# Stick-breaking attention: the third key tile's value product as three rounded products, and the values of heads 5 and 7 one slot later

## The reference

```python
def _stick_breaking(cols):                       # cols: 512 x 3072, eight heads of width 128
    q = _heads(cols[..., :MIX_WIDTH], SB_HEADS, SB_HEAD_DIM) * (SB_HEAD_DIM ** -0.5)
    k, v = ...
    for i in range(seq // BLOCK_Q):              # blocks of 128 queries, keys up to the block's end
        z = jnp.einsum('bhqd,bhkd->bhqk', qb, k[:, :, :end]).astype(jnp.float32)
        u = jnp.where(mask, jax.nn.softplus(z), 0.0)
        a = jnp.where(mask, jnp.exp(z - _rev_cumsum(u)), 0.0)
        outs.append(jnp.einsum('bhqk,bhkd->bhqd', a.astype(v.dtype), v[:, :, :end]))
```

## Time and profile before

| | |
|---|---|
| median of 3 runs | 2968.88 us (2968.79 to 2970.55) |
| the profiled execution | 2968.38 us, its span 2966.7 us |
| PE busy | 2950.7 us, 99% of the span |
| DVE busy | 2253.9 us, 76% |
| ACT busy | 1470.8 us, 50% |
| mean granted clock of PE | 0.999 of full speed |

### The profile page before, as it was taken

How to read it: one execution, slowest core, us unless ns; L and a number is a source line. 1 busy time by engine, 2 the same in 40 slices (tenths; PEclk the granted TensorE clock), 3 DMA queues, 4 the chain that set the end, 5 groups by cost and what they waited for, 6 DMA issues and landing times.

```text
span 2966.7 us, 47938 instructions
## 1 busy us (share of the span) xinstructions
PE 2950.7 (99%) x18733; PEld 2649.9 (89%) x18733; DVE 2253.9 (76%) x2781; ACT 1470.8 (50%) x2158; POOL 60.9 (2%) x148
## 2 busy tenths in 40 slices
PE   9999999999999999999999999999999999999999
PEld 8779999888889999878899998889999888899998
DVE  7979888567659887576598875558898567588884
ACT  4576555455445555344455553226555354365554
POOL 6100000000000000000000000000000000000000
PEclk9999999999999999999999999999999999999999
DMA  6232333341133333311332333223233322233332
GB/s 204 60 96 87 112 113 107 107 142 58 55 101 100 102 104 106 101 57 56 101 100 99 106 101 107 85 71 114 99 102 104 93 85 66 63 114 99 108 98 79
DMA packets 261943, 286.45 MB, mean 97 GB/s; under 512 B 12514, under 2 KB 233888, under 8 KB 261800
## 3 DMA queue, kind: packets, MB, share of 16 engines
q1 hardware_dynamic: 261688, 284.42, 29.9%
q10 hardware_dynamic: 112, 0.02, 0.0%
HBM read 280.21 MB, written 5.78 MB: 96 GB/s over the span
## 4 chain that ended last, share of the span: by engine, by line
PE 93%; DVE 4%; POOL 1%; ACT 1%; issue 1%; DMA 0%; ACTq 0%; POOLq 0%; DVEq 0%; SPq 0%
PE ps L2961 40%; PE ps L2612 14%; PE ps L2614 14%; PE ps L2613 14%; PE ps L3323 1%; PE ps L3324 1%; PE ps L3325 1%; PE ps L3230 1%; PE ps L3290 1%; PE ps L3269 1%; PE ps L3309 1%; PE ps L3311 1%; PE ps L3310 1%; PE ps L3176 1%; PE ps L3165 0%
## 5 line engine op out<-in xcount | busy, mean ns | idle before, releaser
L869 ACT ACTIVATE whi<-raw 128x2048 fp32r<-128x2048 f32 (+2 forms) x144 | 246.5, 1712 | 472.6 <-PE ps L2614 382.4
L1559 DVE TENSOR_TENSOR wlo<-raw,whi 128x2048 fp32r<-128x2048 f32 (+2 forms) x144 | 293.5, 2038 | 220.8 <-ACT whi L869 220.5
L2961 PE MATMUL ps<-th,wh 128*128 128x256 f32 x1600 | 453.7, 284 | 0.6 <-DVE wl L1648 0.5
L2961 PE MATMUL ps<-tl,wh 128*128 128x256 f32 x1600 | 452.7, 283 | 0.0
L2961 PE MATMUL ps<-th,wl 128*128 128x256 f32 x1600 | 452.7, 283 | 0.0
L2612 PE MATMUL ps<-hh,whi 128*128 128x512 f32 x896 | 356.2, 398 | 0.0
L2614 PE MATMUL ps<-hh,wlo 128*128 128x512 f32 x896 | 349.5, 390 | 0.0
L2613 PE MATMUL ps<-hl,whi 128*128 128x512 f32 x896 | 349.2, 390 | 0.0
L2961 PE MATMUL ps<-hh,wh 128*128 128x256 f32 x1200 | 340.1, 283 | 0.1
L2961 PE MATMUL ps<-hh,wl 128*128 128x256 f32 x1200 | 339.6, 283 | 0.0
L2961 PE MATMUL ps<-hl,wh 128*128 128x256 f32 x1200 | 339.6, 283 | 0.0
(11 more groups left out here) (517 smaller groups left out, 6674.4 us busy)
## 6 DMA issues: line engine op xcount, KB each, us to landing
raw<-in_w_ffn_in SPq DMA_DIRECT2D x88, 1024.0 KB, 5.1
raw<-in_w_in SPq DMA_DIRECT2D x59, 1024.0 KB, 5.3
raw<-in_w_ffn_out SPq DMA_DIRECT2D x40, 1024.0 KB, 5.1
raw<-in_w_o SPq DMA_DIRECT2D x32, 640.0 KB, 4.4
raw<-in_w_gate SPq DMA_DIRECT2D x11, 1024.0 KB, 5.4
raw<-in_w_up SPq DMA_DIRECT2D x11, 1024.0 KB, 5.3
raw<-in_w_down SPq DMA_DIRECT2D x10, 1024.0 KB, 5.1
raw<-in_w_out SPq DMA_DIRECT2D x4, 1024.0 KB, 5.1
```

The source lines that it names most:

```text
L869: a.activation(whi[:, slot, 0:n], raw[:, slot, 0:n], ACT.Copy).then_inc(hi_made, 1)
L1559: v.tensor_tensor(wlo[:, u % 2, 0:n], raw[:, u % 2, 0:n], whi[:, u % 2, 0:n].bitcast(F32), ALU.subtract).then_inc(lo_made, 1)
L2961: e = mm(bank(b, HALF), wgt[:, q, w], xx, start=start and k == 0 and m == 0, stop=k == KD // 2 - 1 and m == 2, skip_group_check=True)
```

## The change

The places of the third and the fourth key tile change, so that the third one lies next to the first two; sticks_hi and sticks_lo grow from 896 to 1152 columns and sticks_t shrinks from 384 to 128; v_hi and v_lo hold three key tiles' values in place of two; and the third tile's product goes through `three`. ACT's v_hi so needs all of the pair's values (`values_taken(h // 2, 1)`). sticks_lo and v_lo lie in other places of SBUF. In the table KPV, the fifth head goes from slot 41 to 42, and the seventh from 53 to 54.

```diff
-ZK = {0: 0, 1: 512, 3: 896, 2: 1024}
+ZK = {0: 0, 1: 512, 2: 896, 3: 1152}
...
-KPV = [25, 29, 33, 37, 41, 45, 53, 56]
+KPV = [25, 29, 33, 37, 42, 45, 54, 56]
...
-        sticks_lo = at("sticks_lo", US0, [P, WIDE], F32R)
+        sticks_lo = at("sticks_lo", GS0 + 3072, [P, WIDE], F32R)
...
-        v_hi = at("v_hi", SQB0, [P, 2, 256], F32R)
-        v_lo = at("v_lo", SQB0 + 2048, [P, 2, 256], F32R)
+        v_hi = at("v_hi", SQB0, [P, 3, 256], F32R)
+        v_lo = at("v_lo", GS0, [P, 3, 256], F32R)
...
-                        act.wait_ge(acc_free, g_in(3 * idx) + values_taken(h // 2, 0))
+                        act.wait_ge(acc_free, g_in(3 * idx) + values_taken(h // 2, 1))
...
-                        a.activation(v_hi[:, :, :], vp[h // 2 % 2][:, 0:2, :], ACT.Copy).then_inc(S("v_hi"), 1)
+                        a.activation(v_hi[:, :, :], vp[h // 2 % 2][:, 0:3, :], ACT.Copy).then_inc(S("v_hi"), 1)
...
-                        if j < 2:
+                        if j < 3:
                             three(dst, v_hi[:, j, c], v_lo[:, j, c], sticks_hi[:, keys], sticks_lo[:, keys], j == 0, False)
                             continue
```

More of the change, by code:

```diff
@@ L2398, in stick_slot @@
                         dve.wait_ge(S("v_hi"), NH2 // 2 * idx + h // 2 + 1)
-                        v.tensor_tensor(v_lo[:, :, :], vp[h // 2 % 2][:, 0:2, :], v_hi[:, :, :].bitcast(F32), ALU.subtract).then_inc(S("v_lo"), 1)
+                        v.tensor_tensor(v_lo[:, :, :], vp[h // 2 % 2][:, 0:3, :], v_hi[:, :, :].bitcast(F32), ALU.subtract).then_inc(S("v_lo"), 1)
             def lambda_and_distance():
```

## The result

The changed kernel takes 2992.17 us (median of 6 runs, 2988.56 to 2992.97), the kernel before 2968.97: 1.0075 times, 95% interval 1.0065 to 1.0085, 23.2 us more. The forecast was 2983.4, and 2988.5 the upper end of its range. The direction and the place were as forecast, and 9 us were missing.

The account below looks back on a forecast made before the run. The prediction took PE (TensorE) as the bound, busy 2950.7 of 2966.7 us. Waits 12.5 + wider sticks_lo 3.1 - columns 1.1 = +14.5 us, so 2983.4 us, range 2979.5 to 2988.5.

Parts of the forecast that it names:

- The four waits on L2315: Values of heads 6 and 8, two layers: PE waits for DVE's L2315, 2.48 and 3.76 us, 12.5 in all.
- The wider sticks_lo: DVE's sticks_lo ends 0.27 us later, so the next heads' scores (L3246) start later: 3.1 us in all.
- issue: Gap ahead of the scores, read as a wait for sticks_lo; rival: PE's own sequencer, 2980.3 us, chance 0.12.
- The columns: Third key tile: three rounded products replace one fp32 product on PE, saving 0.07 us 16 times, 1.1 us.
- v_hi, v_lo behind wlo: Wider value conversions, v_lo moving behind wlo for later pairs of heads: cost nothing, 1.6 us of room before stick's turn.
- The rival of the clock: PE's clock falls in head 8's long wait in both layers: 4.8 us more, 2988 us, chance 0.19.
- the longer waits: PE's wait at head 8's values, once in each of two layers: 3.76 us idle each.
- One head's move alone waits: Rival: only the fifth or only the seventh head's move makes PE wait: 2978.4 or 2976 us, chance 0.05.
- DVE has read the bank before: Rival: L2315 of heads 5 and 7 ends before PE arrives: 2967.8, up to 2970.9 us, chance 0.08.

Follow-up runs that it names:

- the filled kernel: The changed kernel with 11 and 16 unread matmuls ahead of PE's waits at heads 6 and 8, keeping PE at work: 2983.22 us.
- the move alone: The kernel before with only the KPV entries of heads 5 and 7 one slot later, product and conversions as before: 2987.01 us, ratio 1.0061.
- the three other kernels with waits: Changed kernel with only head 7's low part early (2978.62 us) or only head 5's (2981.22); kernel before with only KPV changed (2987.01).
- the version with the fp32 product: The changed kernel with early low parts of heads 5 and 7 and the third key tile as one fp32 product of sticks_hi: 2972.01 us.

## Why the prediction was wrong

- The four waits on L2315: right in place and nearly in size. PE's start behind L2315 took 0.26 to 0.30 us and not 0.10, so the waits cost 13.2 and not 12.5. The 12.5 in the table of waits is another measure, from the end of one matmul's record to the next start, and equals the forecast by chance.
- The wider sticks_lo, +3.1: it stands in the trace as worked out, and "issue" was a wait, as its constant distance had said. The columns, -1.1: three records in 0.36 us, as worked out. The runs agree with both (3.2 and 1.2) within their scatter. v_hi, v_lo behind wlo at no cost: PE waits for stick 1.2 us in all, as before.
- The sum, "12.5 + 3.1 - 1.1 = +14.5", is where it failed: it held no term for the clock. Kept at full clock, the changed kernel takes 2983.22 us, against the forecast of 2983.4; the 8.95 us above it are that term, but for some 0.6. That the two agree so closely is in part luck: the filled kernel also spares the later starts that the forecast had left out.
- The rival of the clock had 0.19 and a price of 4.8 us, both too low for the changed kernel. I took the 3.0 us from PE's last work to the fall in the earlier trace rows for the idle time that a fall needs, and so let it happen in the longer waits only, and doubted it even there. The changed kernel's trace shows neither is so: in the fourth layer the clock fell 2.0 us after PE's last work, and around the first layer's sixth head it fell 1.2 us after PE had resumed. The price of one fall was not the miss: 2.4 us in the estimate, 7.2 / 4 = 1.8 in the trace. There were four falls where the rival had two; with the falls in the longer waits only, the move alone, the cost beyond the waits was 18.2 - 13.2 = 5.0, close to the rival's price. The step from a place (PE idle for 2.5 and 3.8 us in a stream of matmuls that had run at 1.00 before it) to "no price" had only one row behind it.
- The rule of the Trainium skill ("TensorE: Matmul & The Clock Gate", section on HAM oscillation), that work after an idle gap starts slow, held in this case in 6 of 12 waits. In 3 more the clock fell 0.5 to 1.3 us after PE had resumed at full speed. Taking the rule for the likeliest case, 2988, would have been nearer.
- "One head's move alone waits" and "DVE has read the bank before" did not happen.

## What to carry to other kernels

Moving a step by a slot moves all that hangs on it on the other engines, and there it may pass an instruction that starts only when the first engine has finished the slot: look in the new order for the reader that now stands behind such an instruction. Where PE runs at full clock without a break, an idle time of a few microseconds is to be priced at more than itself. Here the four waits of 13.2 us cost some 8 more, about three fifths; in the three other kernels with waits it was a third to a half (2.6 us on 7.8, 2.5 on 5.3, 5.0 on 13.2). The repair was an earlier place for two instructions on the engine that was late, not the move back; with it the change costs nothing that can be told from the scatter (+1.9 us), and gains nothing either.

## What the runs showed of the hardware that I had not expected

The clock can fall after PE has resumed (791.0, work since 789.80). It even fell in some executions in a shorter idle time, in the first block, which all these kernels share; this is the window of the kernel before, and the same one of the version with the fp32 product:

```profile
130.00:140.00 10.00, 8.66 (x58) 6.59 (x57) 9.76 (x30) 9.62 (x19) 0.00 (x0) 1.00 0.20 52
```

```profile
130.00:140.00 10.00, 8.65 (x49) 6.58 (x47) 9.76 (x30) 9.61 (x19) 0.00 (x0) 0.86 0.21 52
```

PE idles 1.35 us of this stretch in both, 1.20 of them in one piece, and the clock stayed at 1.00 in the one and fell in the other, while PE stood idle. That may be part of the scatter between runs of one kernel; it was not tried.
